# Loading the weight steps of a two-block transformer in pairs: one transfer of 1 MB where two of 512 KB went

## What is computed

```python
def hybrid_layer(x, c_act, ...):
    mod = c_act @ w_ada + b_ada
    shift, scale, gate = jnp.split(mod, 3, axis=-1)
    h = rms_norm(x, g) * (1.0 + scale[:, None]) + shift[:, None]
    proj = jnp.einsum('bsd,df->bsf', h, w_in)
    ...
    out = jnp.einsum('bsf,fd->bsd', y, w_out)
    return x + gate[:, None] * out

def second_block(x, c, ...):
    for l in range(DEPTH_2):
        mod = c_act @ w_mod[l] + b_mod[l]
        h = x * (1.0 + scale[:, None]) + shift[:, None]
        ...                      # y = attention of h: h @ w_in, then @ w_out
        x = layer_norm(DN_ALPHA * x + gate[:, None] * y, ln_g[l], ln_b[l])
```

## Time and profile before

| | us |
|---|---|
| median of 3 runs | 1427.11 (1427.01 to 1427.54) |
| the profiled execution, its own time | 1428.44 |
| span of the profiled execution, first to last instruction | 1426.6 |
| PE busy in the span | 1402.4 (98%) |
| DVE busy | 1187.7 (83%) |
| ACT busy | 708.7 (50%) |
| PE's share of the chain that ended last | 90% |
| mean DMA rate over the span | 316 GB/s |

### The profile page before, as it was taken

One profiled execution on the slowest core, in us unless ns is written; L12 is line 12 of the kernel. 1 busy time (PEld: TensorE's weight loads), 2 busy tenths in 40 slices (PEclk: granted clock), 3 DMA queues, 4 the chain that ended last, 5 costly groups with the idle time before them and its releaser, 6 DMA issues.

```text
span 1426.6 us, 19790 instructions
## 1 busy us (share of the span) xinstructions
PE 1402.4 (98%) x6894; PEld 1171.0 (82%) x6894; DVE 1187.7 (83%) x1542; ACT 708.7 (50%) x1051; POOL 124.6 (9%) x205
## 2 busy tenths in 40 slices
PE   6999999999999999999999999999999999999996
PEld 4888788888888888888888888888888888888885
DVE  5999999888998789898778789978787877667566
ACT  5655445654445644444456553474345645465440
POOL 1000010103100000110011100000010011110000
PEclk9999999999999999999999999999999999999999
DMA  9999999988996899999977799689789788775762
GB/s 355 416 415 416 411 411 406 346 310 297 412 412 208 303 351 380 400 383 370 342 225 258 237 331 368 238 291 381 257 333 352 246 292 290 232 243 167 270 195 96
DMA packets 101834, 451.00 MB, mean 316 GB/s; under 512 B 11777, under 2 KB 16241, under 8 KB 78193
## 3 DMA queue, kind: packets, MB, share of 16 engines
q1 hardware_dynamic: 73010, 279.09, 53.8%
q0 software_dynamic: 21296, 154.18, 28.1%
q10 hardware_dynamic: 7440, 16.56, 3.2%
HBM read 447.63 MB, written 2.15 MB: 315 GB/s over the span
## 4 chain that ended last, share of the span: by engine, by line
PE 90%; DMA 4%; DVE 4%; issue 2%; ACT 1%; POOL 1%; SPq 0%; DVEq 0%; ACTq 0%; POOLq 0%
PE bank L945 16%; PE bank L947 16%; PE bank L946 16%; PE bank L928 16%; PE bank L926 8%; PE bank L880 3%; PE bank L882 3%; PE bank L881 3%; DMA raw<-in_t_steps 2%; PE bank L1175 2%; PE bank L1133 2%; DVE gw L1768 2%; PE bank L924 1%; PE bank L1151 1%; PE bank L893 1%
## 5 line engine op out<-in xcount | busy, mean ns | idle before, releaser
L1256 ACT CAST w_hi<-raw 128x1024 fp32r<-128x1024 f32 x434 | 455.3, 1051 | 616.5 <-PE bank L947 306.9
L1740 DVE TENSOR_TENSOR w_lo<-raw,w_hi 128x1024 fp32r<-128x1024 f32 x360 | 438.4, 1225 | 173.5 <-ACT w_hi L1256 170.8
L1768 DVE CUSTOM_DVE_ANT_0 gw<-gw,c_act 128x2048 f32<-128x2048 f32 x176 | 401.6, 2283 | 6.3 <-DMA gw<-in_t_ada 6.1
L946 PE MATMUL bank<-w_lo,act_parts 128*128 128x512 f32 x1024 | 398.7, 389 | 0.0
L945 PE MATMUL bank<-w_hi,act_parts 128*128 128x512 f32 x960 | 385.7, 402 | 0.5 <-issue 0.3
L947 PE MATMUL bank<-w_hi,act_parts 128*128 128x512 f32 x960 | 374.8, 390 | 0.0
L928 PE MATMUL bank<-act_parts,w_hi 128*128 128x512 f32 x960 | 338.3, 395 | 0.0
L926 PE MATMUL bank<-act_parts,w_lo 128*128 128x256 f32 x1024 | 276.9, 281 | 0.0
L946 PEld LDWEIGHTS bank<-w_lo,act_parts 128*128 128x128 f32 x1024 | 192.6, 188 | 38.1
L928 PEld LDWEIGHTS bank<-act_parts,w_hi 128*128 128x128 f32 x960 | 180.1, 188 | 39.1
L947 PEld LDWEIGHTS bank<-w_hi,act_parts 128*128 128x128 f32 x960 | 180.2, 188 | 38.8
(11 more groups left out here) (203 smaller groups left out, 1048.0 us busy)
## 6 DMA issues: line engine op xcount, KB each, us to landing
raw<-in_t_steps SPq DMA_DIRECT2D x464, 512.0 KB, 7.1
gw<-in_t_mod POOLq DMA_DIRECT2D x96, 1024.0 KB, 8.4
gw<-in_t_kv_mod POOLq DMA_DIRECT2D x32, 1024.0 KB, 8.4
gw<-in_t_ada SPq DMA_DIRECT2D x30, 1024.0 KB, 10.1
gw<-in_t_ada POOLq DMA_DIRECT2D x18, 1024.0 KB, 8.6
area<-gate_rows ACTq DMA_DIRECT2D x3, 1024.0 KB, 10.7
bias<-forget_sums ACTq DMA_DIRECT2D x16, 192.0 KB, 6.5
area<-in_ln_g ACTq DMA_DIRECT2D x2, 1024.0 KB, 8.0
```

The costliest lines, as they stand in the source:

```text
L946: nc.tensor.matmul(dst, hi, w_lo[:, j % SLOTS, k], start=False, stop=False)
L1256: nc.scalar.copy(w_hi[:, b], raw[:, j % SLOTS]).then_inc(hi_ready, 1)
L1740: nc.vector.tensor_tensor(w_lo[:, j % SLOTS], raw[:, j % SLOTS], w_hi[:, j % LEAD].bitcast(F32), ALU.subtract).then_inc(lo_ready, 1)
L1768: nc.vector.tensor_tensor_reduce(out=w, in0=w, in1=c_act[:].rearrange("p (t n) -> p t n", t=TT), scale=1.0, scalar=0.0, op0=ALU.mult, op1= ...
```

## The change

Two neighbouring steps are laid side by side on the host, so that a partition has 8 KB in one piece, and SP loads both by one transfer of 1 MB, with one semaphore for both (`pair_landed`, 4 of them in place of 8). It does so for all 464 steps: 232 transfers. A pair of steps is loaded when the odd one's slot is free, which is one step later than the even one was loaded before. `HEAD_LEAD` goes from 6 to 7, so that in the first 56 steps the condition on `lo_ready` for a pair is that of its even step before. A row of the modulation that went behind an even step now goes behind the pair.

```diff
-HEAD_LEAD, LEAD_STEPS = 6, 56
+HEAD_LEAD, LEAD_STEPS = 7, 56
...
-        raw_landed = [sem(f"raw_landed{i}") for i in range(SLOTS)]
+        pair_landed = [sem(f"pair_landed{i}") for i in range(SLOTS // 2)]
+        raw_landed = [pair_landed[i // 2] for i in range(SLOTS)]
...
-            def load_step(row, j):
-                sp.dma_start(raw[:, j % SLOTS].rearrange("p k n -> p (k n)"), w_steps[bass.ds(row, P), :]
-                             ).then_inc(raw_landed[j % SLOTS], 16)
+            def load_steps(row, j):
+                s = j % SLOTS
+                sp.dma_start(raw[:, s:s + 2].rearrange("p s k n -> p (s k n)"), w_steps[bass.ds(row, P), :]
+                             ).then_inc(raw_landed[s], 16)
...
-                if k < LEAD_STEPS:
-
-                    wait(sp, lo_ready, k - HEAD_LEAD + 1)
-                wait(sp, half_used, k - SLOTS + 1)
-                load_step(k * P, k)
+                if k % 2 == 0:
+                    if k + 1 < LEAD_STEPS:
+
+                        wait(sp, lo_ready, k + 1 - HEAD_LEAD + 1)
+                    wait(sp, half_used, k + 1 - SLOTS + 1)
+                    load_steps(k // 2 * P, k)
...
-                for j in range(STEPS):
+                for j in range(0, STEPS, 2):
                     k = FRONT_STEPS + j
-                    sp.wait_ge(half_used, i * STEPS + (k - SLOTS + 1))
-                    load_step(i * (STEPS * P) + k * P, j)
+                    sp.wait_ge(half_used, i * STEPS + (k + 1 - SLOTS + 1))
+                    load_steps(i * (STEPS // 2 * P) + k // 2 * P, j)
...
-    return out.reshape(-1, STEP_KT * CHUNK)
+    out = out.reshape(-1, 2, P, STEP_KT * CHUNK).transpose(0, 2, 1, 3)
+    return out.reshape(-1, 2 * STEP_KT * CHUNK)
```

## The result

| | before | after |
|---|---|---|
| median of the runs, us | 1427.11 (5 runs, 1425.57 to 1429.62) | 1436.18 (5 runs, 1434.14 to 1439.10) |
| ratio, 95% interval | | 1.0063 [1.0051, 1.0074] |
| profiled execution, its own time | 1428.44 | 1437.14 |
| its span | 1426.6 | 1435.3 |

The change makes the kernel 9.1 us slower (7.3 to 10.6 by the interval), outside the predicted range (1425.0 to 1432.6) and on the side of the slower rival. The spans differ by 8.7 us, so the two traces show the loss almost in full.

What follows compares the result with a forecast made beforehand. PE, busy for 98% of the span, was taken as the bound. Terms +0.9 - 0.5 + 0.1 + 0 = +0.5 gave 1428.9 us for the profiled execution, 1427.6 us for the median; range 1425.0 to 1432.6.

Steps and rivals of the forecast that it cites:

- the slower rival: Steps 54 to 79: late even steps pass through a full DVE, loss returning each ring turn; 1433.4 us, chance 0.25.
- Behind the front: From 256 us on, 384 steps: later even steps cost PE nothing; 0, bounds 0 and +1 us.
- Rows and steps up to 150 us: Front up to 150 us: positions shift at most one step, PE's later start shrinks weight waits; -0.5 us, bounds 0 and -1.5.
- as long as the queue does not run dry: Up to 150 us: condition for landings to depend on bytes ahead in SP's queue, not issue time; shift at most 1.27 us.
- positions do not add up: Up to 150 us: delays are a shift, not a sum; DVE row waits over 10 us would show otherwise.
- The start: Start of the front: step 2 lands with step 3, so PE's step 2 begins 0.9 us later, bounds 0.75 and 1.27.
- the one of -1.7 to +1.7 for the clock: Just behind PE's idle time at the start: lower-clock piece taken as unchanged, range -1.7 to +1.7 us.
- 150 to 250 us: Front, 150 to 250 us: SP's larger queue share offsets later pairs; +0.1 us, bounds -1 and +1.8.
- The faster one: Front: larger transfers carry more, so weight waits go and the lower-clock piece shrinks; 1423.9 us, chance 0.13.

Runs made afterwards that it cites:

- e10_pairs_where_led: The change with pairs only in steps 80 to 95, 160 to 303 and 320 to 447, single steps elsewhere read from the new layout: 1429.07 us.
- e12_front_but_36_49: The change with pairs only in the front except steps 36 to 49, single steps there and behind the front, read from the new layout: 1430.46 us.
- e0_all_single: The control: the kernel before with no pairs, its 512 KB steps read as 4 KB pieces out of the new layout: 1428.99 us.
- e5_loop_pairs: The change with pairs only in the 384 steps behind the front, single steps in the front read from the new layout: 1434.11 us.
- e3_rows_4k: The change with the old memory layout: still one 1 MB transfer and one signal, but in 4 KB pieces: 1440.38 us.
- e1_late_issue: The kernel before with the change's issue times and SP order, two 512 KB transfers from the old layout, each with its own signal: 1430.25 us.
- e9_late_two_landings: The kernel before with the change's issue times, two 512 KB transfers with two signals, and each cast waiting for both landings: 1441.16 us.

## Why the prediction was wrong

- **Behind the front, "I cost the 384 steps here at 0, with bounds of 0 and +1 us".** This is the step that failed: 5.6 us in the trace, 5.1 to 7.0 in the runs. "The cover is the 4-deep ring and the free 18% of the DMA engines" was true for 288 steps, as `e10_pairs_where_led` shows, and false for a few. I read the lead of all casts from one wait of PE of 0.2 us and from the count of 193 against 14 waits of ACT. Both are sums over the program, and I left out of the earlier trace rows the 3.2 us in 7 waits put down to issue, though I say myself further on that such waits can be waits for weights. The 14 casts that waited for a landing are not the ones either: by the trace of before they are those of steps 128, 134, 135, 178, 179, 208, 210 to 212, 294 to 296, 324 and 325, none of them a step where PE lost time, and 11 of the 14 lie where `e10_pairs_where_led` has its pairs at no cost. The casts that cost the most had waited for nothing: 144 with a lead of 1.9 us and 304 with 0.4, against a delay of 4.0 and 2.4, and with the norm behind them in ACT's list. The size of the delay was nearly right, 2.72 us and the longer transfer; the lead of each cast to set it against, and what stands behind it, were not looked up.
- **"Rows and steps up to 150 us", -0.5 us.** Wrong in sign: from step 15 to step 50 the trace lost 3.6 us (from -0.5 to +3.1), and the front ended with that. That it stood at just -0.5 up to step 39 is no hit: the control, without a pair, stood at -1.1 there. The step that failed is the condition that I had named myself, "as long as the queue does not run dry". It did run dry (369 GB/s against 417), since SP waits at a pair for the odd slot, and the rows behind it wait with it. The other half of the loss, at step 47, is a late pair ahead of other work in DVE's list, which this paragraph has no term for. Whether "positions do not add up" failed too stays open: `e12_front_but_36_49` has a loss with no pair near it, but my own sign for it did not come, for DVE waited for rows 7.3 us in 9 waits up to 150 us, and not more than 10.
- **The start, +0.9 us.** Not seen, and not to be seen in this way: PE's step 2 began at 28.87 us, not near 31.0. The cast of step 2 began at 26.09 after 4.03 us of waiting for its landing, not later than the 26.78 of before, and step 2 ran at once at full clock. Stretches of 28 to 34 us, before and after:

```profile
28.00:34.00 6.00, 3.90 (x10) 3.12 (x11) 5.43 (x8) 3.98 (x5) 0.00 (x0) 0.72 1.01 414
```

```profile
28.00:34.00 6.00, 5.13 (x23) 4.25 (x24) 5.63 (x7) 4.01 (x7) 0.00 (x0) 1.00 1.01 422
```

  The granted clock here is the higher level throughout after (1.00), and partly the lower one before (0.72). But `e0_all_single`, without a pair, has 1.00 as well, and `e5_loop_pairs`, whose front has none either, has 0.63: it varies between executions. And it doesn't matter. The 2.8 us that PE gained at step 2 were 2.0 at step 8 and 0.2 at step 10, because PE waits there for DVE, and DVE for row 6, whose reduction begins at 42.24 us before and at 42.06 after. A term of 0.9, and the one of -1.7 to +1.7 for the clock, were paid out of a stretch that is made up again.
- **150 to 250 us, +0.1.** Right behind step 50, but not shown to be so for the reason given: the loss was 3.2 us at step 63 and 3.1 at step 79. (Step 47 ends at 163 us, within the stretch, but its pair was issued at 145.87.) The transfers landed sooner, 9.2 us after issue where the 512 KB took 11.5, and POOL's rows later, 9.7 for 8.6. In the stretch of the earlier trace rows, 197 to 200 us:

```profile
q1 hardware_dynamic: 101, 0.73, 58.5%
q0 software_dynamic: 79, 0.52, 41.6%
```

  SP's queue had 0.44 of 1.26 MB and has 0.73 of 1.25. So much for 3 us; over the whole 100 us SP's queue moved 21.34 MB where it had moved 21.33. And with 4 KB pieces the transfers landed nearly as soon: 9.4 us after issue in `e3_rows_4k`, 9.5 in `e1_late_issue`. So most of the shorter time came with the later issue, and not with the longer pieces. The place from which the slower rival was to start did not lose there either, or little: from step 50 to 79 nothing in `e9_late_two_landings`, 0.85 us in `e3_rows_4k`. So the hit in this term is in part luck. What the 8 KB pieces do show is on POOL's side: its rows took 9.7 us, and 8.4 to 8.5 in the kernels with late issue and 4 KB pieces.
- **The rivals.** The slower one had 1433.4, the nearest of my times. It had the mechanism (an even step, late with its partner, ahead of other work in an in-order list) but at steps 54 to 79, and with a loss that returns with each turn of the ring. No such return is in the trace: a loss comes once, at a place, and no second one follows a turn of the ring later. The faster one is out: larger pieces may carry more (4.2 us between `e3_rows_4k` and the change, not settled), but the late issue and the coupling together take 13 to 14 us. The Trainium skill ("DMA: Bandwidth & Descriptors", section "Bandwidth") has the rule of 1 MiB a transfer; here the size by itself moved nothing (`e9_late_two_landings` 1441.16 us, `e3_rows_4k` 1440.38). The fixed cost of about 2 us, which the prediction takes from the same page, stands there for transfers that GpSimd issues; the pairs are issued by SP, and no run here measured such a cost.

## What to carry to other kernels

Two buffers under one signal take from the first of them its lead: the later issue and the longer transfer, here 2.72 + 1.3 = 4.0 us at one place and 2.4 at another. Before doing so, list the casts (or whoever reads the buffers) that begin on a landing or within that time behind it, and ask of each what is queued behind it on its engine and on the next one down the chain; an absence of waits on the bounding engine and a mean lead say nothing of these. And where other loads stand behind the pair in one queue, they inherit its wait, so that an argument by positions in a full queue has to show first that it stays full.

## What was unexpected of the hardware

- The length of the contiguous piece may count apart from the size of the transfer: 8 KB pieces landed 1 MB in 8.1 us where 4 KB pieces took 9.1 (500 to 600 us; elsewhere the difference was smaller or none), with about 4 us of the program by the medians. Two transfers in place of one made no difference.
- How two queues that are both full share the engines was not settled. From 197 to 200 us the packets were nearly one for one (100 to 123 before, 79 to 101 after), which would give larger pieces more bytes; but from 360 to 376 us there were 532 of POOL's to 703 of SP's before, and 492 to 364 after, and SP's share of the bytes was 39% before, 43% after and 46% in `e3_rows_4k`, whose pieces are as small as before.
- Pieces of 4 KB at a distance of 8 KB were slower than the same pieces side by side, by 1.9 us [0.4, 3.1] over the program (`e0_all_single`). Why stays open; the kernel also has one more set of semaphores and its loop of loads in other form, and these were not tried alone.
- The start moves between executions: PE's step 2 ended between 31.1 and 36.2 us in the fourteen traces, step 10 between 55.6 and 58.1.
- Still open: the loss at step 113 was read from the trace and not tested alone, and why `e12_front_but_36_49` lost 3.4 us at step 46.
